# Second attention of a two-layer decoder kernel: heads one at a time, or in pairs with three-term products in two PSUM banks

## What is computed

```python
a = h @ w_a                                     # 1024 -> 384 + 256 + 32
c_q, c_kv, k_rope = split(a)                    # c_q and c_kv are then rms-normed
q = (c_q @ w_uq).reshape(S, 16, 64 + 32)        # q_nope, q_rope of 16 heads
kv = (c_kv @ w_ukv).reshape(S, 16, 64 + 64)     # k_nope, v of 16 heads
q_rope, k_rope = rope(q_rope), rope(k_rope)     # k_rope is shared by all heads
s = q_nope @ k_nope.T + q_rope @ k_rope.T       # causal, in blocks of 128 queries
o = softmax(s * 96 ** -0.5) @ v
y = o @ w_o                                     # 1024 -> 1024
```

## Time and profile before

| | us |
|---|---|
| median of 3 runs (lowest to highest) | 1290.66 (1290.02 to 1291.46) |
| the profiled execution | 1292.11 |
| its span in the trace | 1290.3 |
| TensorE busy in the span | 1259.6 (98%) |
| VectorE busy, ScalarE busy | 856.8 (66%), 550.8 (43%) |
| 750 to 800 us of the span: TensorE, VectorE, ScalarE busy | 48.99, 35.73, 31.89 |
| first score matmul of the second attention | 720.76 |
| its last weighted sum begins | 870.17 |
| third tile of its output projection begins | 878.84 |

### The profile page before, as it was taken

One profiled execution on the slowest core, in us unless ns is written; L12 is line 12 of the kernel. 1 busy time (PEld: TensorE's weight loads), 2 busy tenths in 40 slices (PEclk: granted clock), 3 DMA queues, 4 the chain that ended last, 5 costly groups with the idle time before them and its releaser, 6 DMA issues.

```text
span 1290.3 us, 18028 instructions
## 1 busy us (share of the span) xinstructions
PE 1259.6 (98%) x6201; PEld 984.9 (76%) x6201; DVE 856.8 (66%) x1302; ACT 550.8 (43%) x1007; POOL 41.7 (3%) x47
## 2 busy tenths in 40 slices
PE   6999999999999999999999999999999999999997
PEld 4677777677888878788888666668788888888886
DVE  3767666658988888855548776765876666663332
ACT  6644454445533333322235666654643333332222
POOL 2000000003000000000030000000300000000000
PEclk9999999999999999999999999999999999999998
DMA  9633343332556666566532111123233333333332
GB/s 320 183 98 89 126 157 89 130 109 71 176 187 195 194 191 194 159 193 192 153 95 66 36 37 35 34 57 98 74 107 98 97 95 94 93 93 102 90 91 93
DMA packets 237846, 154.44 MB, mean 120 GB/s; under 512 B 38057, under 2 KB 225934, under 8 KB 234714
## 3 DMA queue, kind: packets, MB, share of 16 engines
q1 hardware_dynamic: 237786, 153.63, 39.6%
HBM read 151.47 MB, written 2.14 MB: 119 GB/s over the span
## 4 chain that ended last, share of the span: by engine, by line
PE 86%; DVE 7%; ACT 3%; issue 2%; POOL 0%; DMA 0%; SPq 0%; DVEq 0%; ACTq 0%; POOLq 0%
PE pj L1813 72%; PE ov L2120 3%; PE sc L2064 3%; PE tr L2092 2%; DVE wl L1208 2%; PE sc L2076 1%; ACT wh L766 1%; DVE tmp L1314 1%; DVE nmax L1435 1%; DVE ada_w_sb L1249 1%; ACT tmp L934 1%; PE sc L1928 0%; DVE hl L1302 0%; PE sc L2082 0%; PE sc L1939 0%
## 5 line engine op out<-in xcount | busy, mean ns | idle before, releaser
L1208 DVE TENSOR_TENSOR wl<-raw,wh 128x1024 fp32r<-128x1024 f32 (+2 forms) x212 | 234.6, 1107 | 248.3 <-ACT wh L766 245.1
L766 ACT ACTIVATE wh<-raw 128x1024 fp32r<-128x1024 f32 (+2 forms) x212 | 202.3, 954 | 442.0 <-PE pj L1813 438.9
L1813 PE MATMUL pj<-hh,wh 128*128 128x512 f32 x912 | 364.3, 399 | 3.9 <-issue 2.6
L1813 PE MATMUL pj<-hh,wl 128*128 128x512 f32 x912 | 355.9, 390 | 0.0
L1813 PE MATMUL pj<-hl,wh 128*128 128x512 f32 x912 | 355.3, 390 | 0.0
L1813 PE MATMUL pj<-gh,wh 128*128 128x512 f32 x592 | 236.7, 400 | 3.2 <-DVE gl L1332 2.2
L1813 PE MATMUL pj<-gh,wl 128*128 128x512 f32 x592 | 231.7, 391 | 0.0
L1813 PE MATMUL pj<-gl,wh 128*128 128x512 f32 x592 | 231.3, 391 | 0.0
L1813 PEld LDWEIGHTS pj<-hh,wh 128*128 128x128 f32 x912 | 171.3, 188 | 43.2 <-issue 10.0
L1813 PEld LDWEIGHTS pj<-hh,wl 128*128 128x128 f32 x912 | 171.2, 188 | 36.8
L1813 PEld LDWEIGHTS pj<-hl,wh 128*128 128x128 f32 x912 | 171.6, 188 | 32.1
(11 more groups left out here) (253 smaller groups left out, 1148.8 us busy)
## 6 DMA issues: line engine op xcount, KB each, us to landing
raw<-in_ffn_w_in_dram SPq DMA_DIRECT2D x88, 512.0 KB, 3.8
ada_w_sb<-in_ada_w_dram SPq DMA_DIRECT2D x40, 1024.0 KB, 5.2
raw<-in_ffn_w_out_dram SPq DMA_DIRECT2D x32, 448.0 KB, 3.4
raw<-in_fox_w_in_dram SPq DMA_DIRECT2D x22, 512.0 KB, 4.2
raw<-in_ffn_w_out_dram SPq DMA_DIRECT2D x16, 512.0 KB, 3.7
raw<-in_fox_w_o_dram SPq DMA_DIRECT2D x8, 512.0 KB, 3.7
raw<-in_mla_w_o_dram SPq DMA_DIRECT2D x8, 512.0 KB, 3.6
raw<-in_mla_w_a_dram SPq DMA_DIRECT2D x5, 512.0 KB, 3.8
```

The source lines that it names most:

```text
L766: act.activation(wh[:, n0 % 2, 0:kt, :], (raw_tile(n0) if not per else raw[:, n0 % 2, :, :])[:, 0:kt, :], ACT.Copy).then_inc(w_hi, 1)
L1208: dve.tensor_tensor(wl[:, n0 % 2, 0:kt, :], (raw_tile(n0) if not per else raw[:, n0 % 2, :, :])[:, 0:kt, :], f32(wh[:, n0 % 2, 0:kt, :]), ...
L1813: ins = pe.matmul(bank_[:, :], (wl if term == 2 else wh)[:, s, kt, :], (rl if term == 1 else rh)(kt), start=start and j == 0, stop=stop an ...
```

## The change

The second attention goes in pairs, as the first does. Values of all 16 heads are computed ahead of it, with positions on the partitions: `v_products`, two chunks C_V of 1024 elements a partition, eight tiles of 6 products, copied by ACT into the free room `first_scale`. No value is transposed any more. Per pair there are three chunks (plain queries, 9 products; rotary queries with their swapped twins, 9; keys, 6). All four operands of the scores (plain and rotary queries, keys, rotary key) are split in high and low parts, so that a pair's scores are 2 x 3 terms for two heads over 64 rows each. ACT and DVE each do one 128 x 512 piece for a plain query tile and for a key tile; a rotary tile is rotated by DVE, copied by ACT and its low part taken by DVE. Both heads of a step use the two banks `SC` at once, so a step's scores wait for both exponential sums of the step before. The weighted sum of a pair stands in the next pair's first step behind the transposes and two products. Rotary chunks are loaded in six parts. The loops over pairs are written out. The output projection's `out_fill` does 42 products by the table `MLA_LAST`, 21 of each of its first two tiles. The rotary key gets its high and low part before the first scores, on ACT and DVE, and DVE takes it from PSUM before the last latents' low parts.

```diff
+MLA_AHEAD = 6
+MLA_FILL = (0, 6, 11, 18, 24, 30)
+MLA_LAST = (0, 3, 6, 8, 9, 11, 12, 14, 15, 17, 18, 29, 35, 42)
...
+            for v in range(2):
+                slot_free(C_V + v)
+                for kt in range(KVRT):
+                    sp.dma_start(raw[:, (C_V + v) % 2, QB * kt:QB * kt + QB, :].rearrange("p a (b n) -> p (a b) n", n=HD),
...
+            for t in range(PAIRS):
...
+                for h in range(2):
+                    c0, to = (2 * t + h) * MQ + HD, h * HD
+                    load(n + 1, QRT, uq[:, c0:c0 + ROPE], to, to + ROPE)
+                    load(n + 1, QRT, uq[:, c0 + ROPE // 2:c0 + ROPE], to + ROPE, to + ROPE + ROPE // 2)
+                    load(n + 1, QRT, uq[:, c0:c0 + ROPE // 2], to + ROPE + ROPE // 2, to + HD)
...
 @ ScalarE
+            def mla_step(w):
+
+                t, d = divmod(w, QB)
+                for g in halves(w):
+                    exp(g, U_MLA + g, d, mla_bank(g))
+                if w:
+                    for g in halves(w - 1):
+                        turned(g % 2, g % 8 // 2, R_MLA + g, g % 2)
+                if t and d == 1:
+                    pair_take(t - 1, PAIRS)
+                if t < PAIRS - 1 and d < 3:
+                    split(C_MLA + 3 * t + 5 + d)
+                    (take_nope, take_rope, take_key)[d](t + 1)
 @ VectorE
+            dve.tensor_tensor(kt, bk[HD:MQ, :], rope_sb[HD:MQ, :], ALU.mult).then_inc(kr, 1)
+            dve.tensor_tensor(twin, bk[MQ:P, :], rope_sb[MQ:P, :], ALU.mult).then_inc(ev_d, 1)
+            latents_lo(QRT, KVRT)
+            split(C_KR + 2)
+            dve.wait_ge(kr, 1)
...
+            def mla_step(w):
+
+                t, d = divmod(w, QB)
+                for g in halves(w):
+                    maximum(g, U_MLA + g, d, mla_bank(g))
+                for g in halves(w):
+                    normalise(g, U_MLA + g, d)
+                if t and d == 1:
+                    pair_take(t - 1, PAIRS)
+                if t < PAIRS - 1 and d < 3:
+                    if d == 1:
+                        rotate(t + 1)
+                    if d == 2:
+                        rope_low(t + 1)
+                    split(C_MLA + 3 * t + 5 + d)
+                    if d == 0:
+                        take_nope(t + 1)
+                    if d == 2:
+                        take_key(t + 1)
 @ TensorE
-            EARLY = {C_FOXO: 3 * (DT - 1) + 12, C_MLAO: 3 * (DT - 1) + 12}
+            EARLY = {C_FOXO: 3 * (DT - 1) + 12, C_MLAO: 6 * (DT - 1)}
...
+            def v_products(v):
+
+                s = (C_V + v) % 2
+                for q in range(QB):
+                    k = QB * v + q
+                    if k == 0:
+                        bank_free(T_MLA)
+                    elif k == 1:
+                        pe.wait_ge(ev_d, T_KR + 1)
+                    else:
+                        pe.wait_ge(v_ev, k - 1)
...
+                pe.wait_ge(expd, U_MLA + g)
+                for a, b in ((0, 2), (1, 3)):
+                    for term in range(3):
+                        for h in range(2):
+                            pe.matmul(mla_bank(g + h)[:, 0:nc_], mla_tile(gl if term == 2 else gh, a, t)[rows_of(h), q],
+                                      mla_tile(gl if term == 1 else gh, b, t)[rows_of(h), 0:nc_],
+                                      start=a == 0 and term == 0, stop=False)
...
+            def mla_step(w):
+
+                t, d = divmod(w, QB)
+                mla_scores(w)
+                mla_fill(w, 0)
+                if w:
+                    mla_turn(w - 1)
+                mla_fill(w, 1)
+                if t and d == 0:
+                    mla_weighted(t - 1)
```

More of the change, by code:

```diff
@@ new lines, in _ @@
+            for k in range(QB, 2 * QB):
+                take_v(k)
+            split(C_MLA + 1)
+            take_nope(0)
+            split(C_MLA + 2)
+            take_rope(0)
+            split(C_MLA + 3)
+            take_key(0)
+            split(C_MLA + 4)
+            def mla_step(w):
[10 more added lines that the diff above has]
+                    (take_nope, take_rope, take_key)[d](t + 1)
@@ L1780, in _ @@
[L1780 to L1787 removed]
+            dve.tensor_tensor(kt, kt, twin, ALU.add).then_inc(kr, 1)
+            dve.wait_ge(kr, 2)
+            for part in range(2):
+                dve.wait_ge(kr_hi, part + 1)
+                dve.tensor_tensor(mla_tile(gl, 3, 0)[part * ROPE:(part + 1) * ROPE, :], kt,
+                                  f32(mla_tile(gh, 3, 0)[0:ROPE, :]), ALU.subtract).then_inc(kr_lo, 1)
@@ L1788, in _ @@
+            for w in range(QB * PAIRS):
+                mla_step(w)
+            pair_take(PAIRS - 1, PAIRS)
             dve.wait_ge(gate_ok, 3)
```

392 lines of the change are left out of this document (186 added, 206 removed).

## The result

The changed kernel takes 1298.02 us (median of 4 runs, 1296.56 to 1299.48), the kernel before, beside it on the same chip, 1290.34 (1289.82 to 1291.46): a ratio of 1.0058, 95% interval 1.0046 to 1.0070. It is slower by 7.7 us. The forecast was 1295.8, with a range to 1301.0.

A forecast was written before the change was run, and what follows sets the result against it. TensorE was taken as the bound nearly everywhere (weight products 72% of the span). First scores at 736.1 plus pairs and end put the third output tile at 883.9, not 878.84: 1290.66 + 5.1 = 1295.8 us, range 1288.0 to 1301.0.

The forecast's parts named there:

- TensorE's own work for a pair: Second attention, steady pair: scores 5.1, transposes 1.86, weighted sum 2.3, 24 products 6.2, together 15.5 us.
- The waits of a pair: TensorE idle before the weighted sum 0.48, the 512-column scores 0.95 and the next pair 0.61: 2.04 us, pair 17.54.
- Ahead of the attention: Up to the first scores: norm 1.2 later, 57 more products 13.1, other waits 0.6, late load 0.5; first scores 736.1.
- The late load: The second pair's rotary chunk, released at about 731.3, lands late and holds the first maxima up by 0.5 us.
- The end: From first pair to third output tile, with TensorE standing 2.1 us before that tile: 883.9, before 878.84, +5.1 us.
- From the profiled execution to the median: Whole kernel: the +5.1 us from the traced times was added to the median of before, 1290.66, giving 1295.8 us.
- The clock: Rival: waits at the norm of c_q and output projection drop TensorE's clock; 1297.5 or 1299.2 us; 0.20 with late copies.
- The chains-hide rival: VectorE keeps up, so the waits in a pair's third and fourth steps go; pair under 16.8, 1284.8 us; chance 0.12.
- Half of it: Rival: middle score widths or the order of the takes are off by some 0.4 us a pair; 1292.7 us; chance 0.23.
- the sum waits more: Rival: ScalarE, behind with a split, delays the weighted sum's copies 0.4 us a pair more; 1298.6; 0.20 with clock case.

The follow-up runs named there:

- the variant of before: Kernel before with two extra 512-wide VectorE copies into unused room ahead of the norm of c_q; 1292.67 us, ratio 1.0016.
- the four edits together: Changed kernel with VectorE's low parts a step later, three score banks, sum behind the next scores, low part behind the norm of c_q; 1282.69 us, ratio 0.9942.
- the best: Changed kernel with those four edits, 38 early products, third to sixth value tiles and some splits taken earlier; 1279.50 us, ratio 0.9916.

## Why the prediction was right, and where it was not

**TensorE's own work for a pair, 15.5.** Measured 17.31 - 1.40 = 15.91. The score blocks are 0.91, 1.01, 1.34 and 1.69, 4.95 in all (forecast 1.03, 1.00, 1.37, 1.70, together 5.1); transposes 1.85 (1.86); sum 2.30 (2.3). The mis-sized term is the products: 6.2 in the sum, 6.8 measured for 24 in eight groups. I gave a group 0.1 for its start, after the earlier trace rows. Ahead of transposes that holds (785.76 to 786.54 is 0.78 for three, 0.09 more than its 0.23s), but ahead of a wait the last product counts with its whole recorded 0.40 and not with 0.23, some 0.25 in all. The mean over the eight groups is 0.16. With so few products between other work that counts.

By the Trainium skill (TensorEngine Tiling (Array Packing), Theoretical Speedup) two 64-row tiles should give up to twice the speed. The trace agrees at 512 columns, where a term of both heads takes 0.23, as long as one product over all 128 rows. At 256 columns it takes 0.12, and at 128 no less than that, 0.11 to 0.12: the narrowest step is not cheaper still, as the earlier trace rows had it.

**The waits of a pair, 2.04.** Measured 1.40: 0.28 before the sum (forecast 0.48), 0.61 before the 512 columns (0.95), 0.51 before the next pair (0.61). Places, releasers and mechanism were right and the experiments confirm them: backlog of VectorE, two banks, copies of ScalarE. The maxima start at 10.95 and 15.01 after the pair's first scores, forecast 11.12 and 15.23. The sizes were too high as TensorE's own list was longer. The two errors nearly cancel: 17.31 for 17.54.

**Ahead of the attention.** The wait at the norm is 1.36, forecast 0.18 + 1.2; the fifth value tile 1.19 (1.1), the second pair's first products 1.12 (1.2). First scores 736.76, forecast 736.1, but in that the fall of the clock behind the norm cost some 1.5 that the sum did not have; without a fall there they come at about 735.3 (734.81 in the version with fewer early products, whose norm stands 0.48 earlier). So the term was 0.8 too high; but the profiled execution after stood 0.48 earlier than that of before at 302 us already, which leaves 0.3 for the sum. The late load, priced at 0.5 ahead of the first scores, does not hold them up but the first pair: at 737.03 ScalarE's split, and VectorE's low part and the first maxima behind it, waited for it. The Trainium skill (DMA: Bandwidth & Descriptors, Why small descriptors are slow) gives each small piece a fixed cost; no run here parts that cost from the rest. What the trace shows is the issuing: eight issues of query parts stand on SP for 5.12 us from 730.30 on, ahead of that landing. A load in fewer parts was not tried.

**The end.** First pair 13.47 (13.3), five pairs at 17.31 (17.54), the seventh 19.00 (19.2), the last to the end of the early products 23.7 (24.1), then 3.5 (3.5). New idle time 1.95 (2.1), and the third tile starts 3.04 after the first tile's last product (879.90), as before. Third tile 882.94, forecast 883.9: +4.1 instead of +5.1, and most of the miss are the five pairs.

**From the profiled execution to the median: the step that failed.** I added the difference to the median of before and wrote that its one fall of the clock "is inside the time of before". It is inside the profiled execution, 1292.11, and not inside the median: of the 57 runs of before in the experiments' comparisons 46 lie at 1289.57 to 1291.14 with a mean clock of 0.997 or 0.998, and only 11 at 1291.22 to 1291.87 with 0.995 or 0.996. The nine runs of the changed kernel all have 0.996 or less, and both of its traces have a fall. The profiled execution of before is above even the highest of those 57, for it also stood late: 302.48 at the first norm, where the variant of before, with the same program up to there, stood at 301.78. So the account of the 7.7 us is: 4.0 span against span, with one fall in each (4.5 if both executions stood alike at 302 us); 0.45 around the span; 1.77 by which the profiled execution of before is above its median; 1.46 by which that of the changed kernel is below its own. The last two, 3.2 us, are mostly the clock. By my estimate 0.7 of the 1.77 is that late start, and the changed kernel's profiled execution, some 0.36 later at 302 us than is usual for its variants, would be 1.82 below its median otherwise: 1.07 + 1.82 = 2.9 us. No trace of the kernel before without a fall was taken, so this rests on the mean clocks and on the price of a fall in the changed kernel and its variants, 1.2 to 1.6. The rival "The clock" named the norm and the third output tile; both are seen, and a third place, the wait of 1.55 before the last pair, it did not name. That it happened in the typical run I had given a chance of 0.20, and 1298.02 lies in that rival's stretch (above 1298), just outside the 1293.5 to 1298 that had 0.45. That the number came as near as 2.2 us is in part luck: +5.1 was 1 us too high where the clock was missing.

**Around the span** lies 1.8 us in both profiled executions of the kernel before and its variant, and 2.3 in all those of the changed kernel and its variants. The prediction had no term for it. The loops over pairs are written out in the changed kernel; whether that is the cause was not tried.

**The chains-hide rival** asked for a pair under 16.8. The changed kernel does not have it, but its edits do: 15.87 in the same algorithm, decided by the order of VectorE's list, a third bank and the place of the sum. "Half of it" and "the sum waits more" did not come about, though the second shows once the banks are free (0.61).

## What to carry to other kernels

Find the engine whose own work comes before the step that everyone waits for, and move what nobody needs yet behind it: three edits of order and a third bank took 13.9 us off the span (1.5 of it a fall of the clock that this execution did not have) without one instruction less. Waits in one loop are not independent: price them together, since taking one away may show the next (0.28 to 0.61), and all three gave the whole 1.4. When you add a difference of traces to a median, look first whether the traced execution is a typical one; here half-clock stretches made, by estimate, 2.9 of 7.7 us.

## What the runs showed of the hardware

Apart from the stretch in which every trace ends, each fall of TensorE's granted clock to 0.50 lasted 3.4 us, and each stood behind a wait of TensorE of 1.36, 1.55 or 1.94 to 1.96 us. Its price at one place is steady: from the norm to the first scores the changed kernel and the variants with the same work there take 27.43 to 27.48 us in the six traces with a fall and 25.95 to 26.00 in the four without, so 1.5 us. Behind the first scores of the last pair it cost 1.2, behind the third output tile's wait 1.2 to 1.6. But the length of the wait doesn't decide it. In two executions of the same changed kernel the waits of 1.55 and 1.95 were followed by no fall and by a fall each, the wait of 1.37 in the variant of before by none, in the four edits together the clock stayed at 1.00 behind 1.96, and behind the 1.36 at the norm it fell in six traces and stayed in two. What else decides is open. In each of the three combined versions with all four edits, whose profiled executions have no fall, the runs lie within 1.4 us of each other (1279.29 to 1280.22 for the best); the changed kernel's nine lie within 3.3.
